# A two-block transformer layer stack on one core: 512-column passes in the later layer, and the second block's attention output product split in three passes

## What is computed

```python
# first block, for each of its 2 layers, on 16 + 512 tokens
h = rmsnorm(h_res, norm_gain[l])
u_pool, z_pool, c_q, c_kv, k_rope, z_mla, g_pool, g_mla = split(h @ w_in[l])
y_pool = (pool_mix(u_pool, ...) * silu(z_pool)) @ pool_w_up[l]
y_mla = (mla(c_q, c_kv, k_rope, ...) * silu(z_mla)) @ mla_w_up[l]
merged = sigmoid(g_pool) * y_pool + sigmoid(g_mla) * y_mla
h_res = h_res + merged @ w_out[l]
# after the last layer: x = h_res[:, 16:]
# second block
q, k, v, lru_x, lru_g, gate_pre = split(rms_norm(x, norm1_gain) @ w_in_2)
attn = diff_attention(q, k, v, lam)              # 8 heads of 128 columns
attn = rms_norm(attn, attn_subln_gain) * (1 - lam_init)
y_attn = attn @ w_attn_o
y_lru = (gelu(lru_g) * (rg_lru(conv(lru_x), forward) + rg_lru(conv(lru_x), reverse))) @ w_lru_o
x = x + (sigmoid(ga) * y_attn + sigmoid(gl) * y_lru) @ w_out
x = x + hierarchical_moe(rms_norm(x, norm2_gain), ...)   # 16 experts, top 2
```

## Time and profile before

| | |
|---|---|
| median of 3 runs | 1833.78 us (1833.67 to 1835.75) |
| profiled execution: span | 1830.6 us |
| around the span (median less span) | 3.2 us |
| PE busy | 1762.0 us (96%), 11270 instructions |
| DVE / ACT / POOL busy | 65% / 48% / 18% |
| transfers | 241.46 MB, mean 132 GB/s |

### The profile page before, as it was taken

How to read it: one execution, slowest core, us unless ns; L and a number is a source line. 1 busy time by engine, 2 the same in 40 slices (tenths; PEclk the granted TensorE clock), 3 DMA queues, 4 the chain that set the end, 5 groups by cost and what they waited for, 6 DMA issues and landing times.

```text
span 1830.6 us, 27554 instructions
## 1 busy us (share of the span) xinstructions
PE 1762.0 (96%) x11270; PEld 1504.5 (82%) x11270; DVE 1187.4 (65%) x1704; ACT 875.0 (48%) x1407; POOL 331.4 (18%) x223
## 2 busy tenths in 40 slices
PE   8999999999999999999999999999999989999993
PEld 6998788999998888999999776765568867888882
DVE  5566645554366655544676598586764457888896
ACT  5425444234334444334343365556553246878771
POOL 3333222002243222001000276310010000000001
PEclk9999999999999999999999999999999989999997
DMA  6203112223312202323222210213142359999994
GB/s 188 76 24 99 47 47 79 84 70 116 96 59 75 70 25 69 100 93 98 93 83 80 69 47 24 67 48 99 63 172 93 115 195 346 403 402 404 403 384 173
DMA packets 156104, 241.46 MB, mean 132 GB/s; under 512 B 9593, under 2 KB 101018, under 8 KB 155978
## 3 DMA queue, kind: packets, MB, share of 16 engines
q1 hardware_dynamic: 148602, 212.88, 33.9%
q0 software_dynamic: 4464, 16.25, 2.3%
q10 hardware_dynamic: 2912, 10.55, 1.4%
HBM read 223.41 MB, written 16.25 MB: 131 GB/s over the span
## 4 chain that ended last, share of the span: by engine, by line
PE 51%; DVE 5%; ACT 4%; issue 1%; DMA 1%; POOL 0%; POOLq 0%; ACTq 0%; DVEq 0%
PE acc L1358 15%; PE acc L856 10%; PE acc L1101 9%; PE acc L1126 7%; PE acc L1190 2%; PE acc L1204 2%; PE acc L1221 1%; PE acc L1344 1%; PE acc L1212 1%; PE acc L1086 1%; DVE upad L2681 1%; DVE qk L2681 0%; ACT v L1954 0%; PE acc L1008 0%; DVE qk L2679 0%
## 5 line engine op out<-in xcount | busy, mean ns | idle before, releaser
L856 PE MATMUL acc<-h_split,ring_split 128*128 128x264 f32 x1088 | 308.2, 283 | 0.0
L856 PEld LDWEIGHTS acc<-h_split,ring_split 128*128 128x128 f32 x1088 | 204.3, 188 | 0.0
L856 PE MATMUL acc<-h_split,qk_split 128*128 128x264 f32 x384 | 109.5, 285 | 1.3 <-DVE ring_split L2188 1.3
L856 PE MATMUL acc<-ring_split,qk_split 128*128 128x264 f32 x384 | 108.8, 283 | 0.0
L1126 PE MATMUL acc<-ring_split,h_split 128*128 128x256 f32 x384 | 107.9, 281 | 0.0
L856 PE MATMUL acc<-h_split,krope_split 128*128 128x264 f32 x320 | 93.4, 292 | 1.7 <-POOL ring_split L3010 1.6
L856 PE MATMUL acc<-ring_split,krope_split 128*128 128x264 f32 x320 | 90.7, 284 | 0.0
L2188 DVE TENSOR_TENSOR ring_split<-ring,o_split 128x1024 fp32r<-128x1024 f32 (+1 forms) x32 | 44.8, 1417 | 65.3 <-ACT o_split L1520 65.1
L3120 POOL DMA_INDIRECT latent<-h_rows,rows_of x16 | 18.1, 1129 | 355.8 <-PE acc L1344 214.1
L2188 DVE TENSOR_TENSOR ring_split<-ring,qk_split 128x1024 fp32r<-128x1024 f32 (+1 forms) x56 | 59.4, 1070 | 34.1 <-ACT qk_split L1520 34.1
L2996 POOL TENSOR_TENSOR latent<-latent 128x528 f32<-128x528 f32 x18 | 26.8, 1490 | 300.1 <-ACT latent L1515 299.8
(11 more groups left out here) (597 smaller groups left out, 5741.4 us busy)
## 6 DMA issues: line engine op xcount, KB each, us to landing
ring<-in_w_in SPq DMA_DIRECT2D x64, 1024.0 KB, 5.2
ring<-in_w_expert_gate SPq DMA_DIRECT2D x10, 2048.0 KB, 13.7
ring<-in_w_expert_up SPq DMA_DIRECT2D x10, 2048.0 KB, 13.9
ring<-in_w_expert_down SPq DMA_DIRECT2D x10, 2048.0 KB, 14.7
ring<-in_w_out SPq DMA_DIRECT2D x12, 1024.0 KB, 5.0
y_rows<-gate ACTq DMA_DIRECT2D x16, 512.0 KB, 6.8
hres<-in_w_expert_up SPq DMA_DIRECT2D x3, 2048.0 KB, 12.9
qk<-in_w_expert_down SPq DMA_DIRECT2D x3, 2048.0 KB, 14.5
```

The source lines that it names most:

```text
L856: ins = nc.tensor.matmul(dst[0:rows_, half, 0:HALF], w[:, k, :], x[:, c], start=(k == 0 and i == 0), stop=(k == last and i == 2), skip_gro ...
```

## The change

Three things are changed together.

In the first block's later layer (`on_input()`), everything behind the extra tokens' last use is computed on the 512 input tokens alone, as one pass of 512 columns in one bank and not two of 264: the six query chunks of `c`, `z`, `pg`, `gp`, `yp`, `zm`, `gm`, `ym`, `out`, with the elementwise operations on them (`wanted`, `bank`, `passes`). A memset of the extra tokens in `o` on POOL, and DVE's wait for it, go.

In the second block `ya` becomes a `product3`. The normed attention output goes to a scratch tile and from there ACT writes its rounded copy into `qk` (`onup`) and DVE its remainder into `hres` (`onlow`). Its weights are split like the others, the rounded copy by ACT, the remainder by POOL behind POOL's gate multiplies. With `ya` in the list of jobs, `ga` and `ya` have one place each for rounded weights, and the copy for a `ga` is made one round ahead.

As `hres` is taken, SP stores the residual to DRAM (`x_kept`) ahead of the weights `q2` of the second block, and loads it back ahead of the weights `gl3`, after the last `ya`.

```diff
@@ -307,6 +308,30 @@
         X_BY_ACT = (2, 5, 7)
+        def on_input():
+
+            return n.layer == LAYERS - 1
+
+        def wanted(x, narrow=True):
+
+            return x[:, META:T] if narrow and on_input() else x.rearrange("p (a t) -> p a t", a=2)
+
+        def bank(slot, narrow=True):
+
+            return acc[:, slot, 0, :] if narrow and on_input() else acc[:, slot, :, 0:HALF]
+
+        def passes(dst, x, narrow=True):
+
+            if narrow and on_input():
+                return [(dst[:, 0, :], x[:, META:T])]
+            return [(dst[:, half, 0:HALF], x[:, half * HALF:(half + 1) * HALF]) for half in range(2)]
+
+        NARROW = ("z", "pg", "gp", "yp", "zm", "gm", "ym", "out")
+
+        def narrow_job(label):
+
+            return label[0] in NARROW or (label[0] == "c" and label[1] < QC)
+
         ident, mask = const[:, K_IDENT:K_IDENT + P], const[:, K_MASK:K_MASK + P]
@@ -319,6 +344,7 @@
         y_up = [latent_split[:, c, 0:S] for c in range(DC)]
         y_low = [zp_split[:, c, 0:S] if c < PG else o_split[:, c - PG, 0:S] for c in range(DC)]
         m2_up = [qk_split[:, c, 0:S] for c in range(DC)]
+        on_up, on_low = m2_up, [hres_split[:, c, 0:S] for c in range(DC)]
         m2_low = [work_split[:, c, 0:S] for c in range(DC)]
         logits_row = v[:, 0, :]
         squared_tok = [flat[:, i * D:(i + 1) * D] for i in range(QT)]
...
@@ -572,7 +600,7 @@
                   + [(("v2w", g, j), f"v{g}", j) for g in range(4) for j in range(2)]
                   + [(("lx", c), f"lx{c // 2}", c % 2) for c in range(DC)]
                   + [(("lg", c), f"lg{c // 2}", c % 2) for c in range(DC)]
-                  + [(("ga", m), f"ga{m // 2}", m % 2) for m in range(DC)]
+                  + [x for m in range(DC) for x in ((("ga", m), f"ga{m // 2}", m % 2), (("ya", m), f"ao{m // 2}", m % 2))]
                   + [(x, f"{'gl' if x[0] == 'gl' else 'lo'}{x[1] // 2}", x[1] % 2) for x in gl_yl]
                   + [(("out2", m), f"xo{m // 2}", m % 2) for m in range(DC)])
         job_no2 = {x[0]: i for i, x in enumerate(JOBS_2)}
@@ -595,7 +623,7 @@
             return weight2(name, of)[:, :, j * P:(j + 1) * P]
-        LOW_BY_POOL = [job_no2["lx", c] for c in range(4, DC)]
+        LOW_BY_POOL = [job_no2["lx", c] for c in range(4, DC)] + [job_no2["ya", m] for m in range(DC)]
         def job_done(i):
@@ -718,6 +746,13 @@
             in_slot = {}
             for name in GRANULES2:
                 slot = place2[name]
+                if name == "q2":
+                    sp.wait_ge(dve_made, at(dve_made, ("h2low", DC - 1)))
+                    sp.dma_start(x_kept, xr).then_inc(x_away, 16)
+                elif name == "gl3":
+                    sp.wait_ge(psum_filled, at(psum_filled, ("ya", DC - 1)))
+                    sp.wait_ge(x_away, 16)
+                    sp.dma_start(xr, x_kept).then_inc(x_back, 16)
                 if slot in in_slot:
                     sp.wait_ge(psum_filled, at(psum_filled, spent_by(in_slot[slot])))
                 else:
...
@@ -850,10 +883,10 @@
                 for k in range(last + 1):
                     if before:
                         before(k)
-                    for half in range(2):
-                        c = slice(half * HALF, (half + 1) * HALF)
-                        for i, (w, x) in enumerate(((w1, up[k]), (w1, low[k]), (w0, up[k]))):
-                            ins = nc.tensor.matmul(dst[0:rows_, half, 0:HALF], w[:, k, :], x[:, c],
+                    narrow = narrow_job(label)
+                    for (to, of_up), (_, of_low) in zip(passes(dst, up[k], narrow), passes(dst, low[k], narrow)):
+                        for i, (w, x) in enumerate(((w1, of_up), (w1, of_low), (w0, of_up))):
+                            ins = nc.tensor.matmul(to[0:rows_], w[:, k, :], x,
                                                    start=(k == 0 and i == 0), stop=(k == last and i == 2),
                                                    skip_group_check=True)
                 done(ins, label)
...
@@ -1257,11 +1289,8 @@
                     lru(2 * m)
                     lru(2 * m + 1)
                 product3(("ga", m), dve_evacuated, h2_up, h2_low)
-                if m % 2 == 0:
-                    weights2_in(f"ao{m // 2}")
-                product2(("ya", m), dve_evacuated, [columns2(f"ao{m // 2}", m % 2)[:, k, :] for k in range(DC)],
-                         lambda k: q2[:, k, :],
-                         before=(lambda k: pe.wait_ge(dve_made, at(dve_made, ("on", k)))) if m == 0 else None)
+                product3(("ya", m), dve_evacuated, on_up, on_low,
+                         before=(lambda k: pe.wait_ge(dve_made, at(dve_made, ("onlow", k)))) if m == 0 else None)
                 if m == 0:
                     lru(0)
                     lru(1)
...
@@ -1911,6 +1943,11 @@
                 act.wait_ge(act_evacuated, at(act_evacuated, ("o2", len(items2) - 1)))
                 made(nc.scalar.activation(tmp[c % 2], q2[:, c, :], ACT.Square), ("sqo", c))
+            def normed_upper(c):
+
+                act.wait_ge(dve_made, at(dve_made, ("on", c)))
+                upper(on_up[c], tmp[2 + c % 2], ("onup", c))
+
             for c in range(2):
                 output_squares(c)
             for c in range(DC + LAG):
@@ -1920,13 +1957,16 @@
                 if c >= LAG:
                     i = c - LAG
                     if i >= 2:
-                        act.wait_ge(dve_made, at(dve_made, ("on", i - 2)))
+                        normed_upper(i - 2)
+                        act.wait_ge(dve_made, at(dve_made, ("onlow", i - 2)))
                     elif i == 0:
                         act.wait_ge(pool_made, at(pool_made, ("conv", DC - 1)))
                     root2(("oss", i), tmp[2 + i % 2], P)
                     if i + 2 < DC:
                         output_squares(i + 2)
+            for c in range(DC - 2, DC):
+                normed_upper(c)
             act.wait_ge(act_evacuated, at(act_evacuated, ("lg", DC - 1)))
             for c in range(DC):
                 act.wait_ge(pool_made, at(pool_made, ("lgs", c)))
@@ -1940,7 +1980,7 @@
                 if u:
                     act.wait_ge(dve_made, at(dve_made, ("lru_in", u - 1)))
                 else:
-                    act.wait_ge(dve_made, at(dve_made, ("on", DC - 1)))
+                    act.wait_ge(dve_made, at(dve_made, ("onlow", DC - 1)))
                 b = V_BA - V_BG + 8 * d + c
                 nc.scalar.activation(tmp[0], acc[:, slot, 0, :], ACT.Tanh, scale=0.5, bias=half_bias[:, b:b + 1])
                 b += V_BI - V_BA
@@ -1975,6 +2015,7 @@
                 elif m % 2 == 0:
                     lru_upper(m - 2)
                     lru_upper(m - 1)
+                weights2_upper(job_no2["ya", m] + 2)
                 if m % 2 == 1:
                     for u in range(4 * (m // 2), 4 * (m // 2) + 4):
                         act.wait_ge(dve_made, at(dve_made, ("lru_f", u)))
...
@@ -2650,15 +2694,18 @@
             weights2_lower(EARLY2 + 1)
             for c in range(-LAG, DC):
-                if c + LAG < DC:
+                if c + LAG < DC - 1:
                     weights2_lower(job_no2["lg", c + LAG] + 2)
                 if c < 0:
                     continue
                 inverse2(("oss", c), 2 + c % 2)
                 if c == 0:
                     chain(ts(small[:, 13:14], vec2[:, V_SUB:V_SUB + 1], 1.0 - LAM_INIT, None, ALU.mult))
-                made(stt(out=q2[:, c, :], in0=q2[:, c, :], scalar=small[:, 13:14], in1=tmp[2 + c % 2],
-                         op0=ALU.mult, op1=ALU.mult), ("on", c))
+                x = tmp[2 + c % 2]
+                made(stt(out=x, in0=q2[:, c, :], scalar=small[:, 13:14], in1=x, op0=ALU.mult, op1=ALU.mult), ("on", c))
+                if c == 0:
+                    dve.wait_ge(x_away, 16)
+                lower(on_low[c], x, on_up[c], ("onlow", c), ("onup", c))
             def lru_unit(u):
                 d, c = lru_units[u]
@@ -2724,6 +2771,7 @@
                     for u in range(4 * (m // 2), 4 * (m // 2) + 4):
                         lru_scan(u)
                         if u == 2 * DC - 3:
+                            weights2_lower(job_no2["gl", 1])
                             gate_in(("gl", 0), DC)
                             weights2_lower(job_no2["gl", 0] + 2)
             for c in range(DC - 2, DC):
@@ -2742,6 +2790,7 @@
                 made(tt(merged[:, m, :], merged[:, m, :], gate[:, m % 2, 0:S], ALU.add), ("mg2", m))
                 weights2_lower(job_no2["yl", m] + 2)
                 merged2_lower(m)
+            dve.wait_ge(x_back, 16)
             for m in range(DC):
                 evacuated(stt(out=xr[:, m, :], in0=result2(("out2", m)), scalar=0.5, in1=xr[:, m, :],
                               op0=ALU.mult, op1=ALU.add), ("out2", m))
...
@@ -3106,6 +3153,8 @@
                 pool.wait_ge(act_evacuated, at(act_evacuated, ("lg", c)))
```

(2 more changed lines are left out.)

116 lines of the change are left out of this document (59 added, 57 removed).

## The result

| | before | changed |
|---|---|---|
| median of the runs, side by side | 1834.8 us (1833.7 to 1836.3, 4 runs) | 1873.7 us (1869.1 to 1875.6, 4 runs) |
| ratio, 95% interval | | 1.0212 (1.0197 to 1.0227) |
| span of the profiled execution | 1830.6 us | 1873.6 us |
| its mean granted clock | | 0.970 |
| PE / DVE / ACT / POOL busy | | 1765.0 / 1198.5 / 886.2 / 350.8 us |

The forecast was 1862 with a range of 1849 to 1873: the sign is right, the size is 12 us short, and the median lies 0.7 us above the range.

A forecast was written before the change was run, and what follows sets the result against it. PE was taken to bound the unbroken stretches, ACT and DVE the norm's end and recurrence. Terms −12.5 + 9.4 + 15.8 + 15.5 = +28 us on 1833.8 gave 1862 us, range 1849 to 1873.

The forecast's parts named there:

- Part 1: Later layer of the first block: 512-column passes in place of 264-column ones save PE time, −12.5 us.
- bound of -9.5: Later layer: the narrow-pass gain if half is lost for the 22 products where PE sometimes waits.
- Part 2: Norm loop: PE stands 3.1 us before each of lg5, lg6, lg7, as DVE's lowering waits for ACT; +9.4 us.
- Rival (c): Gate products and ga0: PE's clock falls after stands, 2 us lost per spell, total 1873 us; chance 15%.
- Part 3: Norm tail, lg7 to first lru evacuation: slower chunks, a DVE stand beside POOL, gelu after the last reciprocal; +15.8 us.
- Part 4: Recurrent loop: ACT copies, DVE lowerings and POOL blocking add +15.5 us, ends 6.5 and 21; ya's PE saving counts 0.
- ACT's copy: Recurrent loop: eight added weight copies on ACT, 0.95 us each, on the chain in rounds 0, 1, 3, 5, 7.
- the block: Recurrent loop, even rounds: POOL's weight lowering holds up a DVE step, 2.1 us more.
- Part 5: Residual's store and reload: hidden behind other work, costed at nothing; 3 us each if the cover fails.
- (a): Whole kernel: PE is the bound, so the change is faster, 1811 us; 5% together with a half-way case at 1828.
- (b): Norm tail and loop: POOL does no harm, part 4 at 6.5 and 2.1 off part 3, 1851 us; chance 20%.

The follow-up runs named there:

- n1: The kernel before with the narrow 512-column passes of the later layer alone: 1821.1 us, ratio 0.9925.
- n3: The changed kernel with DVE's lowerings of the normed attention output made two chunks later in the norm loop: 1852.6 us.
- n4: The changed kernel with three float32 filler passes on PE ahead of each of lg5, lg6 and lg7: 1866.2 us.
- n10: n3 with four float32 filler passes on PE ahead of ga1, ga3, ga5 and ga7: 1848.9 us.
- n5: The changed kernel with POOL's lowering of ya's weights cut to 8 of 128 columns, PE passes unchanged in number and length: 1870.6 us.
- n6: The changed kernel with ACT's weight copy for the next even ya put behind the square roots in rounds 1, 3 and 5: 1873.2 us.
- n7: The changed kernel with both the edits of n5 and n6 (short POOL lowering, later ACT copy): 1863.6 us.
- n9: n7 with four float32 filler passes on PE ahead of ga1, ga3, ga5 and ga7: 1856.0 us.
- n11: n1 with ga's weight copies and lowerings made one round ahead instead of two: 1827.8 us.
- n2: The changed kernel with the later layer back in 264-column passes, three-pass ya and parked residual kept: 1884.3 us.
- n8: The changed kernel with eight float32 filler passes on PE ahead of ga1, ga3, ga5 and ga7: 1880.5 us.

## Why the prediction was right in sign and 12 us short

**Part 1 held.** -12.5 forecast, -12.8 in the trace, -14.2 in n1's medians. (The ten other profiles with the narrow layer have the end of its unbroken stretch at 869.0 to 872.6, so the trace's figure is good to 2 us.) The bound of -9.5 was not needed: passes beside which PE sometimes waits gave their gain too.

**Part 2, half of it.** The stall is as worked out: 4.1 us from the end of a gate product to the next instead of 0.86, 9.8 in all (forecast 9.4), and n3 takes it away. Missing is what the stall does to PE's clock. "by the rows of this stretch alone, where PE never stood for 3 us between gate products, the sum has no such term, and I leave it out" is the step that failed, a cost put at nothing: the change makes the very gaps that the stretch lacked. Rival (c) had it, at 2 us a spell; the three products lost 7.4 in this profile and 3.6 to 6.7 in six others. n4 shows cause and size. The Trainium skill, page "TensorE: Matmul & The Clock Gate", section "What's actually happening", has the throttled state as the default, released by activity. The trace agrees: 0.66 granted in the 10 us that hold the first gap.

**Part 3 held to the tenth**: 34.0 us from the end of `lg7` to the first `lru` evacuation, with DVE's 2.69 us row at the place and of the kind expected. The Trainium skill, page "SBUF — State Buffer", section "SBUF: two separate sides", calls the port pair that DVE and GpSimd (POOL) share an exclusive lock. The rows agree: a lowering of 0.69 and a scan of 1.23 us took 2.69 and 3.47 when they began beside a POOL operation of 2.33 and 2.39.

**Part 4 failed in its overlap**, "PE needs 2 × 15.9 us for a pair of rounds, the ACT and DVE chain 32.4 [...], so the 1.3 us that each `ya` saves lies beside the chain: 0". It compares totals, and at the full clock. Within the pair, `ga3` waits for weights that are now lowered one round before their use, so PE's 13.86 us for `ga3` and `ya3` begin in the middle of the pair and end after DVE is ready for them. The costs that the forecast did have were found: in the odd round ACT's copy (0.95 forecast, 1.06) and DVE's first multiply beside POOL (1.01 to 1.14 instead of 0.67; 0.6 forecast), in the even one the block (2.1 forecast; 3.47 instead of 1.29 is 2.2, on the pair of lowerings and not on the step behind them). What was not in the sum is the 1.59 us wait for PE: pair 37.6 and not 36. Over the loop: three pairs 15.6 us, 2.9 up to the first table load, 2.3 from the last on, 20.8.

Behind this wait stands the clock again, and that changes the lesson. `ga3` and `ya3` take 13.86 us after a stand of 4.62 us and 11.1 at the full clock, 2.8 less, which is more than the 1.59 us wait. n10 keeps the clock and changes nothing else against n3: the pair is 36.0, the forecast's own figure, and the loop 5.0 us shorter. So, by n10, nearly all of the 5.3 us that part 4 was short is the same term that part 2 left out, and rival (c) did not have it either: it counted only the gate products and `ga0`. What the block and the copy cost can't be said one by one: in the loop n5 gains 2.5 us, n6 0.9, n7 9.7 and, with the clock kept, n9 15.1. The 5.7 us by which n9's loop is still longer than before were not taken apart.

**Part 5 held**: the end of `lg4` lies 309.3 us after the end of the unbroken stretch, against 309.1. The 1.8 us after the loop are no sign of the reload: n1, which has no reload, took 365.6 us there, and all the profiles lie between 362.9 and 366.3. **Of the rivals**, (a) is out, (c) is true in its place and joins the forecast's own terms, and (b), that POOL does no harm, is answered in halves: in the tail the harm is 2.0 us, in the loop POOL's shorter lowering alone gains 2.5, as PE's path is nearly as long. That (c)'s 1873 is also the time measured is luck: its 11 us were for the gate products and `ga0`. The gate products have 7.4, and the rest of the excess is mostly the loop's, which (c) did not price.

One figure of the range does not follow: part 1 in full, part 4 low and part 3 less 2 give 1851, not 1849.

The sum of the trace is -12.8 + 0.2 + 17.2 + 15.8 + 20.8 + 1.8 = +43.0; the forecast's was +28.2. Of the 14.8 between them 7.4 are the clock in the norm loop, 5.3 the loop with PE on its chain at a low clock, 1.8 the end, and 0.3 the rest. The 7.4 are the most of seven profiles, and the profiled run was the longest of its four, which goes some way to explain why this sum is 4.1 above the medians.

## What to carry to other kernels

A ratio of totals ("PE 31.8 us a pair, the chain 32.4") says nothing of order: ask when the input of each product is ready, and what waits for its end. Where a change makes PE stand, price the products behind the stand at the low clock too, in every place where it stands. A list of jobs that share a few places in turn halves everybody's lead when a second job is put into it, so reprice the jobs that the diff doesn't name. And where two paths lie abreast, remove both before you judge either; here n5 and n6 read alone would have said that POOL and ACT hardly matter in the loop.

## What the hardware showed that I had not expected

PE's clock fell where I had assumed it would not: behind stands of 3.2 us between bursts of 5.6 us, and in n11 behind one of 2.85. The burst itself then takes 5.8 to 8.6 us, and which it is changes from run to run. That may be why the changed kernel's runs spread over 6.4 us and those of n1 over 1.9, but it isn't shown: n2, with the same gaps, spread over 2.0. Filling the gap with idle passes kept the 2.4 GHz (three products in 17.6 us; `ga3` and `ya3` in 11.1 instead of 13.86). n8's filler was longer than the gap, and cost 1.3 us a pair. A float32 pass over 512 columns is recorded as two instructions of 0.44 us, 0.88 together, against 0.2314 for an fp32r pass: `ya` in three fp32r passes (5.6 us) is shorter on PE than in one float32 pass (7.0), and all the same the kernel is slower with it.
